# A hybrid decoder layer on one core: the local attention with heads paired over the key groups, the values as the stationary operand, and another order of VectorE's work

## The chip, the cores and the metric

The kernel runs on 1 core of one Trainium2 chip. The metric is the device time of one execution in microseconds (us), the median of three runs.

## The reference

One decoder layer on 256 tokens of width 1024. A gated linear attention (GLA) and a local attention (called SWA below) read the same normalised input; their outputs are gated, added and projected, and a mixture of 32 experts, 4 of them for each token, follows. The change is in the local attention:

```python
# q: 16 heads of 64, k and v: 2 key heads of 64, each shared by 8 query heads; window w = 128
scores = jnp.einsum('bnqhgd,bnkhd->bnhgqk', qb, kband) * (d ** -0.5)
scores = jnp.where(valid, scores, -jnp.inf)
m = jnp.maximum(jnp.max(scores, axis=-1, keepdims=True), sink)
p = jnp.exp(scores - m)
denom = jnp.sum(p, axis=-1, keepdims=True) + jnp.exp(sink - m)
out = jnp.einsum('bnhgqk,bnkhd->bnqhgd', p / denom, vband)
...
y_b = swa_with_sinks(q, k, v, sinks) @ w_swa_out
mixed = jax.nn.sigmoid(gate_a) * y_a + jax.nn.sigmoid(gate_b) * y_b
```

All numbers are float32. The dense products take each operand in two rounded parts (`_R` tiles) and make three products of them.

## The kernel before, in words

**Order of the program.** Each engine has its own queue, written out by hand, and the engines meet at semaphores. TensorE (PE) works through 19 blocks of dense products (`BLOCKS`), each in two units of weights (`kh` 0 and 1), each unit in two halves. SP loads a unit (`wblk`, 1 MB) once the unit five before it has been multiplied; ScalarE makes its high part (`split`), VectorE or GpSimd its low part (`rest`, or line 495 on GpSimd). From `gla_o` and `sw_out` on, SP also loads chunks of expert weights (`wexp`, 2 MB each, 192 in all) into the ring's tail. Then the experts run, 6 chunks for each; a chunk's place is filled again when TensorE has used it (`chunk_used`).

**The local attention** is cut in 8 groups (`NGRP`): for each of two blocks of 128 tokens (`i`), four groups of four heads (`g4`). Groups 0 to 3 have one tile of 128 keys, groups 4 to 7 two. Its steps are hooks inside the dense blocks 5 to 9. The hook of slot `n` runs `values(n - 2)`, `probs_t(n - 1)`, `scores(n)`, and after it TensorE goes on with dense products:

- `scores`: four products of 64 rows (the head width), two heads side by side on the upper and lower rows of the array, into PSUM banks 4 and 5.
- VectorE's `swa_mask` scales, masks, takes the maximum; ScalarE's `swa_exp` takes exponentials and their sums.
- `probs_t`: the probabilities are transposed, 4 or 8 transposes, and copied from PSUM to `PTS` by ScalarE and VectorE (`swa_pt`).
- `values`: for each head and key tile one product with the probabilities as the stationary operand (128x128) and the values as the moving one (64 columns), line 697, into bank 3.
- VectorE's `swa_out` adds up the denominator (line 1400), takes the reciprocal (1401) and multiplies (1404) into the token-major tile `SQR`.

After the last group `attention_t` transposes `SQR` with 16 transposes (`transpose16`, line 609) in block 10, and ScalarE and VectorE take high and low parts (`OB2`) for block `swao0`. VectorE's iteration `n` runs `swa_out(n - 2)`, `swa_pt(n - 1)`, `swa_mask(n)`, then evacuations of dense banks (line 1258), `rest` and GLA steps.

## Time and profile before

| | |
|---|---|
| median of 3 runs | 1206.51 us (1206.43 to 1206.67) |
| the profiled execution | 1206.25 us, its span 1204.4 us |
| granted TensorE clock | 0.999 |
| busy: PE, DVE, ACT, POOL | 1126.6, 378.2, 269.0, 148.8 us |
| memory read | 446.58 MB, 372 GB/s over the span |

How to read it: PE is TensorE, DVE is VectorE, ACT is ScalarE, POOL is GpSimd, SP the engine that issues most transfers. Busy time of PE is modelled (matmuls overlap), so the starts in the chain tell more than busy shares. The chain of waits is the one that ended last, followed back from the end: where two rows of it follow each other without a gap, the engine was never waiting. A float32 product is two instructions in the trace, a float32 transpose one.

### The profile page before, as it was taken

What the parts mean: (1) busy time and instruction counts of PE and PEld (TensorE: products, weight loads), DVE (VectorE), ACT (ScalarE), POOL (GpSimd) and SP (SyncE); (2) the same over time, 40 slices, a digit from 0 to 9 for tenths busy, and PEclk for the clock granted to TensorE, in tenths of its full rate; (3) what the DMA queues carried; (4) which work ended last, traced back from release to release, by engine and by line L of the source; (5) the groups of instructions that cost most, each with busy time, mean ns of one, the idle gap of its engine ahead of it and who ended that gap; (6) DMA issues with size and microseconds to landing.
All of it is one profiled execution on the core that took longest, in us unless ns stands there. A gap on an engine that the chain in (4) does not pass through costs nothing.

```text
span 1204.4 us, 17839 instructions
## 1 busy us (share of the span) xinstructions
PE 1126.6 (94%) x7411; PEld 558.7 (46%) x7411; DVE 378.2 (31%) x654; ACT 269.0 (22%) x410; POOL 148.8 (12%) x108
## 2 busy tenths in 40 slices
PE   7999999999999999999999999999999999998896
PEld 5988999984333333333333333333333333333332
DVE  6878744855211212211111111111111221111112
ACT  5465746332111111111111111111111111111112
POOL 6645543561000000000000000000000000000000
PEclk9999999999999999999999999999999999999999
DMA  7644336789999999999999999999999999999994
GB/s 295 215 172 158 106 141 243 295 309 375 414 393 426 429 429 426 428 429 429 428 428 428 429 429 429 428 428 429 428 429 428 428 429 429 428 428 429 428 429 204
DMA packets 35827, 448.14 MB, mean 372 GB/s; under 512 B 4160, under 2 KB 4288, under 8 KB 6576
## 3 DMA queue, kind: packets, MB, share of 16 engines
q1 hardware_dynamic: 34992, 445.99, 88.9%
q0 software_dynamic: 368, 1.24, 0.3%
q8 instruction: 26, 0.43, 0.1%
q10 hardware_dynamic: 432, 0.42, 0.1%
q14 instruction: 9, 0.07, 0.0%
HBM read 446.58 MB, written 1.05 MB: 372 GB/s over the span
## 4 chain that ended last, share of the span: by engine, by line
PE 51%; DMA 41%; DVE 4%; POOL 1%; ACT 1%; issue 1%; SPq 0%; DVEq 0%; ACTq 0%
DMA ring<-wexp 40%; PE PS L843 28%; PE PS L574 12%; PE PS L836 3%; PE PS L828 2%; POOL slot_R L495 1%; PE PS L904 1%; PE PS L697 1%; DVE slot_R L1203 1%; DMA ring<-wblk 1%; PE PS L671 1%; PE PS L820 0%; PE PS L684 0%; PE PS L609 0%; PE PS L899 0%
## 5 line engine op out<-in xcount | busy, mean ns | idle before, releaser
L843 PE MATMUL PS<-ring,SQ 128*64 128x512 f32 x2016 | 454.8, 596 | 58.0 <-DMA ring<-wexp 56.7
L843 PEld LDWEIGHTS PS<-ring,SQ 128*64 128x64 f32 x2016 | 138.3, 136 | 348.9 <-issue 227.8
L843 PE MATMUL PS<-ring,PTG 128*64 128x512 f32 x1024 | 226.8, 595 | 0.0
L843 PEld LDWEIGHTS PS<-ring,PTG 128*64 128x64 f32 x1024 | 70.7, 137 | 152.2 <-issue 133.2
L495 POOL TENSOR_TENSOR slot_R<-ring,slot_R 128x512 fp32r<-128x512 f32 (+1 forms) x80 | 124.2, 1584 | 96.2 <-ACT slot_R L948 96.2
L1641 DVE TENSOR_SCALAR SQ<-PS 128x512 f32<-128x512 f32 x32 | 22.1, 692 | 360.8 <-PE PS L843 360.8
L1149 ACT ACTIVATE SQ<-SQ 128x512 f32<-128x512 f32 x32 | 20.2, 630 | 494.0 <-DVE SQ L1641 494.0
L1632 DVE TENSOR_TENSOR PTG<-TAB,GRX 128x128 bf16<-128x128 f32 x32 | 9.3, 292 | 332.8 <-PE PS L891 332.8
L574 PE MATMUL PS<-slot_R 128*128 128x256 f32 (+1 forms) x296 | 92.3, 312 | 0.0
L948 ACT ACTIVATE slot_R<-ring 128x2048 fp32r<-128x2048 f32 (+1 forms) x38 | 71.6, 1888 | 41.5 <-DMA ring<-wblk 24.5
L836 PE MATMUL PS<-PTG,BRW 64*128 64x512 f32 x264 | 74.2, 640 | 0.7 <-ACT PTG L1157 0.7
L574 PE MATMUL PS<-HT_R,slot_R 128*128 128x256 f32 x400 | 73.3, 285 | 0.3 <-DVE GRX L1258 0.3
L1157 ACT ACTIVATE PTG<-PS 128x512 f32<-128x512 f32 x32 | 19.1, 597 | 208.2 <-PE PS L843 208.2
L574 PEld LDWEIGHTS PS<-HT_R,slot_R 128*128 128x128 f32 x400 | 62.3, 192 | 1.2 <-issue 0.7
L574 PE MATMUL PS<-slot_R,HT_R 128*128 128x512 f32 (+1 forms) x192 | 58.1, 378 | 0.7 <-POOL slot_R L495 0.7
L828 PEld LDWEIGHTS PS<-PTG,SQR 128*128 128x128 bf16 x1056 | 46.1, 98 | 26.0 <-issue 26.0
L574 PEld LDWEIGHTS PS<-slot_R 128*128 128x128 f32 x296 | 56.4, 191 | 2.9
L828 PE MATMUL PS<-PTG,SQR 128*128 128x64 bf16 x1056 | 50.0, 193 | 0.0
L828 PE MATMUL PS<-PTG,SIG 128*128 128x64 bf16 x528 | 47.8, 193 | 0.0
L1203 DVE TENSOR_TENSOR slot_R<-ring,slot_R 128x2048 fp32r<-128x2048 f32 (+1 forms) x17 | 43.5, 2560 | 8.3 <-ACT slot_R L948 8.1
L1149 ACT ACT_TABLE_LOAD x32 | 41.1, 1283 | 5.6 <-issue 5.1
L574 PEld LDWEIGHTS PS<-slot_R,HT_R 128*128 128x128 f32 x192 | 35.2, 188 | 9.2 <-POOL slot_R L495 1.1
(278 smaller groups left out, 991.3 us busy)
## 6 DMA issues: line engine op xcount, KB each, us to landing
ring<-wexp SPq DMA_DIRECT2D x190, 2048.0 KB, 33.3
ring<-wblk SPq DMA_DIRECT2D x36, 1024.0 KB, 4.8
EXT<-wexp SPq DMA_DIRECT2D x1, 2048.0 KB, 9.4
GRX<-wexp SPq DMA_DIRECT2D x1, 2048.0 KB, 12.2
BRW<-brow SPq DMA_DIRECT2D x7, 256.0 KB, 5.0
ring<-wskv SPq DMA_DIRECT2D x2, 768.0 KB, 10.3
GRX<-x SPq DMA_DIRECT2D x2, 512.0 KB, 4.3
out<-EXT SPq DMA_DIRECT2D x3, 256.0 KB, 2.0
```

The source lines that it names most:

```text
L495: last = nc.gpsimd.tensor_tensor(w_unit(u, True)[:, part], w_unit(u)[:, part], h_unit(u, True)[:, part].bitcast(F32), ALU.subtract)
L574: last = mm(dst, left(k, a), right(k, b), start=(kh == 0 and k == 0 and a + b == 0 and first), stop=(kh == 1 and k == KH - 1 and b == 1), ...
L671: last = mm(PS[:, 4 + hh % 2, (hh // 2) * SEQ:(hh // 2) * SEQ + ns], qT[p0:p0 + HD, h // 2, i * P:(i + 1) * P], KTT[p0:p0 + HD, h // (QH / ...
L697: last = mm(PS[:, 3, hh * HD:(hh + 1) * HD], PTS[:, n % 2, hh, st * P:(st + 1) * P], KVRAW[:, st, P + kv * HD:P + (kv + 1) * HD], start=(s ...
L828: last = mm(PS[:, 7, k * SLOTS:(k + 1) * SLOTS], XP[n // TT][:, n % TT, k * P:(k + 1) * P], SEL[:, n % TT, :], start=(n == 0), stop=(n == ...
L836: last = mm(bk(2 * i + n), SELT[rows, i * P:(i + 1) * P], Y[rows, :], start=False, stop=True, skip_group_check=True)
L843: last = mm(PS[g * SLOTS:(g + 1) * SLOTS, b, :], lhsT, rhs[:, g * 512:(g + 1) * 512], start=start, stop=stop)
L948: fn(h_unit(u, True), w_unit(u), ACT.Copy).then_inc(hi_ready, 1)
L1149: fn(SGM, GLU, ACT.Sigmoid, scale=ALPHA).then_inc(sgm_ready, 1)
L1157: fn(Y, bk(6), ACT.Copy).then_inc(y_ready, 1)
L1203: v.tensor_tensor(w_unit(u, True), w_unit(u), h_unit(u, True).bitcast(F32), ALU.subtract).then_inc(lo_v, 1)
L1641: v.tensor_scalar(GLU, bk(4), LIMIT, None, ALU.min).then_inc(glu_ready, 1)
```

## The change

Heads are paired over the two key heads: group `g4` now holds heads 2·g4 and 2·g4+1 of each key head, by a permutation of weight columns on the host. The score products are the same in number and size. The values become the stationary operand (128x64), and the transposed probabilities of two heads move (256 columns), the two key heads on the left and right halves of the array's columns. The output is then feature-major and needs no transposes at the end; but its division by the denominator needs the reciprocals spread over 64 features and transposed as well: VectorE writes them into `KD`, TensorE transposes them (two for each group), ScalarE copies the result to `KTT` (`swa_rb`), and VectorE multiplies. The keys no longer need a second copy, which takes away two transposes and four small writes.

```diff
-                kv = g4 // 2
-                for hh in range(HG):
-                    for st in range(i + 1):
-                        last = mm(PS[:, 3, hh * HD:(hh + 1) * HD], PTS[:, n % 2, hh, st * P:(st + 1) * P],
-                                  KVRAW[:, st, P + kv * HD:P + (kv + 1) * HD], start=(st == 0), stop=(st == i))
+                for st in range(i + 1):
+                    for kv in range(2):
+                        mm(PS[kv * HD:(kv + 1) * HD, 3, 0:2 * P], KVRAW[:, st, P + kv * HD:P + (kv + 1) * HD],
+                           PTS[:, n % 2, kv, 2 * st * P:2 * (st + 1) * P], start=(st == 0), stop=(st == i))
+                pe.wait_ge(sw_rd, n + 1)
+                for j in range(2):
+                    last = nc.tensor.transpose(PS[:, 3, (2 + j) * P:(3 + j) * P], KD[:, j, P:2 * P], ident)
                 last.then_inc(sw_o, 1)
...
-            def attention_t():
-
-                pe.wait_ge(sw_out, NGRP)
-                transpose16(lambda i, k: SQR[:, i, k * P:(k + 1) * P], obt_full)
-
             def gla_scores():
 
-                pe.wait_ge(obt_hi, 4)
-                pe.wait_ge(obt_lo, 4)
...
+            def swa_rb(n):
+                act.wait_ge(sw_o, n + 1)
+                if n:
+                    act.wait_ge(sw_out, n)
+                fn(KTT[:, 1, :], PS[:, 3, 2 * P:4 * P], ACT.Copy).then_inc(sw_rb, 1)
...
             for n in range(NGRP + 1):
+                if n >= 2:
+                    swa_rb(n - 2)
                 if 0 <= n - 1:
                     swa_pt(n - 1)
...
+            def swa_denominator(n):
+                q = n % 2
+                dve.wait_ge(sw_exp, n + 1)
+                link(v.tensor_tensor(S_DEN[q], S_SUM[q], S_ES[q], ALU.add))
+                link(v.reciprocal(S_RD[q], S_DEN[q]))
+                v.tensor_copy(KD[:, :, P:2 * P].rearrange("p j (v d) -> p j v d", v=2),
+                              S_RD[q].rearrange("p (v j) -> p j v", v=2).unsqueeze(3).broadcast_to([P, 2, 2, HD])).then_inc(sw_rd, 1)
+
             def swa_out(n):
                 i, g4 = n // (NGRP // TT), n % (NGRP // TT)
-                q = n % 2
-                dve.wait_ge(sw_exp, n + 1)
-                if n >= 2:
-                    dve.wait_ge(sw_out, n - 1)
-                link(v.tensor_tensor(S_DEN[q], S_SUM[q], S_ES[q], ALU.add))
-                link(v.reciprocal(S_RD[q], S_DEN[q]))
-                dve.wait_ge(sw_o, n + 1)
...
+                dve.wait_ge(sw_rb, n + 1)
+                v.tensor_tensor(OB_RAW[:, 2 * g4:2 * g4 + 2, i * P:(i + 1) * P],
+                                PS[:, 3, 0:2 * P].rearrange("p (j t) -> p j t", j=2),
+                                KTT[:, 1, :].rearrange("p (j t) -> p j t", j=2), ALU.mult).then_inc(sw_out, 1)
...
-                if n - 2 >= 0:
-                    swa_out(n - 2)
-                if 0 <= n - 1 < NGRP - 1:
+                if 0 <= n - 1 < NGRP:
                     swa_pt(n - 1)
                 if n < NGRP:
                     swa_mask(n)
+                if 0 <= n - 1 < NGRP:
+                    swa_denominator(n - 1)
+                if n - 2 >= 0:
+                    swa_out(n - 2)
...
-            dense(10, {(0, 1): [attention_t]})
+            dense(10)
```

The high and low parts of the attention's output are now each one instruction of 2048 columns from SBUF to SBUF (four of 512 from PSUM before), and block `swao0` waits for them.

On TensorE, slot 7 (in block 8) before. L574 are dense products, L697 the values, L684 the transposes of probabilities, L671 the scores; the numbers are output rows by columns.

```order
L574 MATMUL PS<-slot_R 128x512
L574 MATMUL PS<-slot_R,HT_R 128x512
L697 MATMUL PS<-GRX,ring 128x64 x8
L684 MATMUL PS<-TAB,ring 128x128 x8
L671 MATMUL PS<-KTT,SQ 128x256 x4
L574 MATMUL PS<-HT_R,slot_R 128x256 x2
```

The same place in the changed kernel (L575 dense, L694 values, L698 transposes of the reciprocals, L683 and L670 as L684 and L671).

```order
L575 MATMUL PS<-slot_R 128x512
L575 MATMUL PS<-slot_R,HT_R 128x512
L694 MATMUL PS<-ring,GRX 64x256 x4
L698 MATMUL PS<-TAB,GRX 128x128 x2
L683 MATMUL PS<-TAB,ring 128x128 x8
L670 MATMUL PS<-KTT,SQ 128x256 x4
L575 MATMUL PS<-HT_R,slot_R 128x256 x2
```

Eight products of 64 columns became four of 256, and two transposes came in behind them.

On VectorE, iteration 6 before: L1400, L1401 and L1404 are `swa_out(4)`, L1391 is `swa_pt(5)`, L1377 to L1386 are `swa_mask(6)`, L1258 the evacuation of a dense bank.

```order
L1400 TENSOR_TENSOR SM<-SM 128x4
L1401 RECIPROCAL SM<-SM 128x4
L1404 TENSOR_TENSOR SQR<-PS,SM 128x2x2x64
L1391 COPY ring<-PS 128x512
L1377 SCALAR_TENSOR_TENSOR ring<-PS,TAB 128x512 x2
L1382 TENSOR_REDUCE SM<-ring 128x4
L1384 TENSOR_TENSOR SM<-SM,ROW 128x4
L1385 TENSOR_SCALAR SM<-SM 128x4
L1386 TENSOR_TENSOR SM<-ROW,SM 128x4
L1258 TENSOR_TENSOR GRX<-PS,BRW 128x512
```

The same iteration in the changed kernel: L1396, L1397 and L1398 are `swa_denominator(5)`, L1404 is `swa_out(4)`, L1263 the evacuation.

```order
L1391 COPY ring<-PS 128x512
L1377 SCALAR_TENSOR_TENSOR ring<-PS,TAB 128x512 x2
L1382 TENSOR_REDUCE SM<-ring 128x4
L1384 TENSOR_TENSOR SM<-SM,ROW 128x4
L1385 TENSOR_SCALAR SM<-SM 128x4
L1386 TENSOR_TENSOR SM<-ROW,SM 128x4
L1396 TENSOR_TENSOR SM<-SM 128x4
L1397 RECIPROCAL SM<-SM 128x4
L1398 COPY GRX<-SM 128x2x128
L1404 TENSOR_TENSOR SQR<-PS,KTT 128x2x128
L1263 TENSOR_TENSOR GRX<-PS,BRW 128x512
```

The multiplication of group 4 moved from ahead of the mask to behind it, and a denominator (of the group after it) stands between the two.

## Rows read from the trace of the kernel before

**Rows 1.** Windows: busy us (instructions) of each engine, clock, DMA share, GB/s.

```profile
core 0: us, PE busy (x) PEld busy (x) DVE busy (x) ACT busy (x) POOL busy (x), PEclk, DMA share, GB/s
...
120.00:150.00 30.00, 30.00 (x224) 27.52 (x222) 22.36 (x37) 24.02 (x43) 15.55 (x13) 1.00 0.32 106
...
270.00:300.00 30.00, 28.33 (x231) 14.64 (x231) 14.26 (x52) 7.75 (x15) 4.64 (x4) 1.00 0.93 375
800.00:1100.00 300.00, 274.76 (x1778) 100.83 (x1778) 59.86 (x117) 36.44 (x53) 0.00 (x0) 1.00 1.01 428
```

**Rows 2.** Chain that ended last, attention stage: start us, us, what.

```profile
72.21 5.47 PE PS L574 x24
77.67 0.65 PE PS L671 x8
78.32 5.67 PE PS L574 x24
83.99 0.44 PE PS L684 x4
...
90.76 0.84 PE PS L697 x8
...
107.31 1.06 PE PS L671 x8
...
126.19 5.66 PE PS L574 x24
131.85 1.73 PE PS L697 x16
133.58 0.88 PE PS L684 x8
...
157.38 1.75 PE PS L609 x16
```

**Rows 3.** The same chain, 197 to 220 us.

```profile
197.68 14.41 PE PS L574 x120
...
212.11 6.90 DMA ring<-wblk
```

**Rows 4.** The same chain, expert stage.

```profile
287.31 10.30 PE PS L843 x48
...
302.38 10.88 PE PS L843 x52
...
500.40 31.69 DMA ring<-wexp
```

**Rows 5.** The same chain, 297 to 304 us.

```profile
299.68 1.06 PE PS L836 x4
300.74 0.59 PE PS L904 x4
```

**Rows 6.** The same chain: a step of one pass at 287.09 us.

```profile
287.09 0.22 PE PS L891 x2
```

**Rows 7.** Timeline of VectorE, 129 to 135 us: start, us, instruction [idle before].

```profile
129.01 1.15 DVE L1385 TENSOR_SCALAR SM<-SM 128x4 f32<-128x4 f32 x1
130.07 0.15 DVE L1386 TENSOR_TENSOR SM<-ROW,SM 128x4 f32<-128x4 f32 x1
...
130.74 0.67 DVE L1400 TENSOR_TENSOR SM<-SM 128x4 f32<-128x4 f32 x1
131.44 0.18 DVE L1401 RECIPROCAL SM<-SM 128x4 f32<-128x4 f32 x1
134.05 0.42 DVE L1404 TENSOR_TENSOR SQR<-PS,SM 128x256 f32<-128x256 f32 x1 [2.43 <-PE PS L697]
```

**Rows 8.** Timeline of GpSimd, 125 to 135 us.

```profile
125.10 5.02 POOL L495 TENSOR_TENSOR slot_R<-ring,slot_R 128x512 fp32r<-128x512 f32 x4 [4.38 <-ACT slot_R L948]
130.09 1.29 POOL L481 TENSOR_TENSOR GRX<-GRX,SIG 128x512 f32<-128x512 f32 x1
```

**Rows 9.** Groups of ScalarE instructions by form, 77 to 165 us: busy us, mean ns.

```profile
L1022 ACT ACTIVATE ring<-PS 128x256 f32<-128x256 f32 x4 | 1.5, 376 | 1.8 <-PE PS L684 1.8
```

More of the change, by code:

```diff
@@ L228, in program @@
         OB2 = (feature(SQ_R), feature(SQR_R))
+        OB_RAW = feature(SQR)
         OA2 = (feature(GV_R), feature(GR_R))
@@ L649, in _ @@
             pe.wait_ge(krot_ready, TT)
-            for g in range(2):
-                for i in range(TT):
-                    last = nc.tensor.transpose(PS[:, 3, (2 * g + i) * P:(2 * g + i + 1) * P],
-                                               KD[:, i, g * P:(g + 1) * P], ident)
+            for i in range(TT):
+                last = nc.tensor.transpose(PS[:, 3, i * P:(i + 1) * P], KD[:, i, 0:P], ident)
             last.then_inc(kt_full, 1)
@@ L668, in scores @@
                 for hh in range(HG):
-                    h = HG * g4 + hh
-                    p0 = (h % 2) * HD
-                    last = mm(PS[:, 4 + hh % 2, (hh // 2) * SEQ:(hh // 2) * SEQ + ns],
-                              qT[p0:p0 + HD, h // 2, i * P:(i + 1) * P],
-                              KTT[p0:p0 + HD, h // (QH // 2), 0:ns], start=True, stop=True)
+                    kv, j = hh % 2, hh // 2
+                    rows = slice(kv * HD, (kv + 1) * HD)
+                    last = mm(PS[:, 4 + kv, j * SEQ:j * SEQ + ns], qT[rows, 2 * g4 + j, i * P:(i + 1) * P],
+                              KTT[rows, 0, 0:ns], start=True, stop=True)
                 last.then_inc(sw_s, 1)
@@ L683, in probs_t @@
                     for st in range(i + 1):
-                        last = nc.tensor.transpose(PS[:, 6 + hh // 2, (2 * (hh % 2) + st) * P:(2 * (hh % 2) + st + 1) * P],
-                                                   SS[:, n % 2, hh, st * P:(st + 1) * P], ident)
+                        c = (2 * st + hh % 2) * P
+                        last = nc.tensor.transpose(PS[:, 6 + hh // 2, c:c + P], SS[:, n % 2, hh, st * P:(st + 1) * P], ident)
                 last.then_inc(sw_t, 1)
@@ L769, in _ @@
             for i in range(13, NB - 1):
+                if BLOCKS[i] == "swao0":
+                    pe.wait_ge(obt_hi, 1)
+                    pe.wait_ge(obt_lo, 1)
                 dense(i)
@@ L1069, in high_t @@
                     fn(dst[:, 2 * a:2 * a + 2, :], PS[:, 4 + a, :].rearrange("p (k t) -> p k t", k=2), ACT.Copy).then_inc(done, 1)
+            swa_rb(NGRP - 1)
             act.wait_ge(gr_ready, 3)
@@ L1074, in _ @@
             split(23)
-            high_t(OB2[0], obt_full, obt_hi)
+            act.wait_ge(sw_out, NGRP)
+            fn(OB2[0], OB_RAW, ACT.Copy).then_inc(obt_hi, 1)
             split(24)
@@ L1270, in rotate @@
                 link(v.tensor_tensor(t2, src[:, :, 1, :], s, ALU.mult))
-                for d in dst:
-                    last = v.tensor_tensor(d[:, :, 0, :], t1, t2, ALU.subtract)
-                link(last)
+                link(v.tensor_tensor(dst[:, :, 0, :], t1, t2, ALU.subtract))
                 v.tensor_tensor(t1, src[:, :, 1, :], c, ALU.mult)
                 link(v.tensor_tensor(t2, src[:, :, 0, :], s, ALU.mult))
-                for d in dst:
-                    last = v.tensor_tensor(d[:, :, 1, :], t1, t2, ALU.add)
-                last.then_inc(done, 1)
+                v.tensor_tensor(dst[:, :, 1, :], t1, t2, ALU.add).then_inc(done, 1)
                 dve.wait_ge(done, i + 1)
@@ L1352, in _ @@
                 evacuated(dve, 4 + i)
-                kd = KD[:, i, :].rearrange("p (h c x d) -> p h c x d", h=2, c=2, x=2)
                 rotate(KVRAW[:, i, 0:P].rearrange("p (h x d) -> p h x d", h=2, x=2),
-                       [kd[:, :, c] for c in range(2)], 2, i, krot_ready)
+                       KD[:, i, 0:P].rearrange("p (h x d) -> p h x d", h=2, x=2), 2, i, krot_ready)
             dve.wait_ge(z_ready, GH)
@@ L1692, in units, with head_pairs @@
         return w.reshape(2, KH, P, -1).transpose(0, 2, 1, 3).reshape(2, P, -1)
+    def head_pairs(a):
+        return a.reshape(2, QH // 2, HD, -1).transpose(1, 0, 2, 3).reshape(QH * HD, -1)
+    sq = slice(at["sq"], at["sq"] + QH * HD)
+    w_in, b_in = w_in.copy(), b_in.copy()
+    w_in[:, sq] = head_pairs(w_in[:, sq].T).T
+    b_in[sq] = head_pairs(b_in[sq])[:, 0]
     def columns(name):
@@ L1696, in columns @@
             w = f[{"gl": "w_gla_out", "sw": "w_swa_out", "wo": "w_out"}[name[:2]]][0]
+            if name[:2] == "sw":
+                w = head_pairs(w)
             n = int(name[-1]) * BW
```

34 lines of the change are left out of this document (12 added, 22 removed).

## The prediction

> **What bounds the kernel now.** I read the windows first, then the chain of waits from end to end, then the timelines of the engines in the attention stage. In the expert stage the transfers fill the DMA engines: share 1.01 at 428 GB/s, while PE is busy 275 of 300 us [rows 1], and the chain there is a product, then a transfer of over 30 us that it waited for, again and again [rows 4]. Ahead of the experts, from 270 to 300 us, the DMA share is 0.93 already. The chunks are issued as TensorE frees their places, so that stage is a block of fixed length whose start hangs on TensorE's arrival. The attention stage is another matter. The chain stays on PE there and its rows touch: the scores begin at 77.67 and last 0.65, the next dense row begins at 78.32 and lasts 5.67, the transposes begin at 83.99 [rows 2]. TensorE does not wait once from 70 to 212 us; then a transfer of weights, which was itself issued when TensorE had freed a unit at 212.1, takes 6.90 us [rows 3]. VectorE (22.36 of 30 us) and ScalarE (24.02) are well used beside it but end no wait [rows 1]. So a microsecond that TensorE saves before 160 us moves every later release with it, transfers of weights and chunks included, and the end too; what it must wait for is added in full.
>
> **The values, from the nearest rows.** A float32 product of 512 columns on half of the array's columns costs 10.30 / 24 = 0.429 us when two halves run at the same time: the row has 48 instructions, two for each product [rows 4]. The new products have 256 columns, so a pair (both key heads) takes 0.429 us. That is the stream alone. The rows also show a price for entering and leaving a split array. The scores (four products, 64 rows each) cost 0.65 us with 128 columns and 1.06 with 256: the stream is 0.41 for 128 columns and 0.24 is left over on entry [rows 2]. The dense row behind them takes 5.67 where the one behind plain transposes takes 5.47: 0.20 on leaving [rows 2]. Four transposes cost 0.59 behind a split product [rows 5] and 0.44 otherwise [rows 2]: 0.15. For entering the shape used here, the expert row of 52 instructions takes 10.88; 48 of them are worth 10.30, and four one-pass products 0.44 (0.22 for two [rows 6]), which leaves 0.14. I take 0.14 + 0.15 = 0.29 us for each group, since these two rows have the very shapes (columns halved; transposes behind it), with 0 and 0.44 as the ends.
>
> The Trainium skill, TensorEngine Tiling (Array Packing), Key Properties, says that a change of tiling mode drains the engine; the 0.14 to 0.24 us above agree. The same page, When to Use Tiling, advises exactly this swap for a moving side of 64 columns, at up to twice the speed; halving the old values and charging no drain gives 5.1 us there, where the rows give far less.
>
> Two transposes of the reciprocals are 0.22 us for each group (0.44 for four [rows 2]). Groups 0 to 3: 0.43 + 0.29 + 0.22 = 0.94 us in place of 0.84 [rows 2], 0.10 more each. Groups 4 to 7: 0.86 + 0.29 + 0.22 = 1.37 in place of 1.73 [rows 2], 0.36 less each. Sum over the eight: 0.4 - 1.44 = **-1.0 us**. The final 16 transposes go: **-1.75** [rows 2]. Two key transposes go: **-0.22**. TensorE's own work is 3.0 us less. With drains at 0.44 it is 1.8 less, with none 5.3 less.
>
> **The other engines.** ScalarE gets eight copies of 256 elements (0.38 us each [rows 9]) ahead of a copy that waits for later transposes anyway, hidden in its waits for VectorE. Scores, exponentials and probability copies keep their sizes. The high and low parts of the output wait for `sw_out` now, with blocks 10 to 14 ahead of their use: hidden. Fewer writes of rotated keys and a half-size key copy are off the path. No transfer is added.
>
> **The new wait.** `values(n)` cannot begin until `swa_out(n - 1)` has emptied bank 3. That was the first thing in VectorE's iteration; now it stands behind the mask and the denominator. Take TensorE's slot 7, which begins with `values(5)` at 131.85 [rows 2], 0.18 us earlier in the changed kernel by the terms above (0.22, less 4 x 0.10, plus 0.36): 131.67. VectorE ends the mask of group 6 at 130.22 [rows 7], and this end is tied to the scores. Then come the sum, the reciprocal (0.18), the spread copy (new; at most the 0.42 of a multiplication of 256 elements, at least a fraction of it) and the multiplication, 0.42 [rows 7]. Undisturbed, with 0.15 for the sum, as for its like at 130.07 [rows 7], and 0.1 between them, that is 131.5: 0.2 us to spare. But GpSimd works from 125.10 to 131.38 [rows 8], and VectorE's small instructions stretch at its borders: 1.15 us for one at 129.01, and the sum at 130.74 takes 0.67 and ends at 131.41, just behind GpSimd's instruction [rows 7, 8]. The Trainium skill, SBUF — State Buffer, SBUF: two separate sides, calls that an exclusive lock held for a whole instruction; the trace agrees with its 0.67 against 0.15. Put the new sum there and it too ends at 131.41. With 0.18, 0.42, 0.42 and 0.1 the bank is free at 132.5: TensorE waits **0.85 us**, and everything behind it, GpSimd's and ScalarE's next steps too, is that much later. In slots 1 to 5 GpSimd works less and the mask of one key tile is shorter; in slots 8 and 9 VectorE has no later mask or GpSimd is idle again, so I count one such wait. Its ends are 0 (no lock met) and 2.1 (the spread copy meets the next GpSimd instruction of 1.29 as well).
>
> **Sum.** -3.0 + 0.85 = -2.2 us. The profiled execution would go from span 1204.4 to 1202.2 (1206.25 to 1204.1 in all); its time is 0.26 under the median, so the median goes from 1206.51 to **1204.4 us**. A measurement of this kernel tells 0.2%, 2.4 us, from no change, so this is just within it.
>
> **The rivals.**
> - VectorE is in time: no wait of more than some tenths. For it: only the phase of GpSimd's instructions decides, and it shifts with ScalarE's splits. Against it: the stretched rows stand exactly there. -3.0 gives 1203.5 us, faster. Chance 0.32.
> - The drains cost nothing here, because the wait for the reciprocals or the loads cover them: -5.3, 1201.2 us, faster. Against it: each of four kinds of rows shows a drain. Chance 0.06. The advice in the Trainium skill, TensorEngine Tiling (Array Packing), When to Use Tiling, comes to the same time: 10.28 us of values halved is 5.1, less 1.76 of new transposes, plus 1.97 removed.
> - The late wait is larger (two locks, or drains at the upper end): -1.8 + 2.1 at worst, 1204.8 to 1206.8 us, no difference. Chance 0.09.
> - The halves do not run together: a pair costs 0.86. Groups 0 to 3 cost 0.53 more, 4 to 7 0.50 more, in all +4.1 - 2.0 + 0.85 = +3.0, 1209.5 us, slower. Against it: the expert rows run at 0.429. Chance 0.03.
> - The other side: VectorE's longer way back (mask, denominator, multiplication) is late in every slot of two key tiles, and TensorE waits at each `values`. It turns slower once these waits add up to 5.4 us (2.4 + 3.0), 1.1 in each of the five slots 5 to 9, for instance 1209.5 us at 6. It would need both locks in most slots, and GpSimd is busy only half of the time (15.55 of 30 [rows 1]). Chance 0.05.
>
> **How the numbers follow.** The forecast (a wait of 0.6 to 1.3 us, all within 0.2%) has 0.45. Faster by over 0.2%: 0.32 + 0.06 = 0.38. Slower: 0.03 + 0.05 = 0.08. Within: 0.45 + 0.09 = 0.54. The range takes in the forecast, the case without a wait (down to 1203.2) and most of the larger waits (up to 1206.2), about 0.84 together; the forecast's own range is 1203.9 to 1204.8.
>
> **What would show it.** In the chain after: the values with the two transposes 0.94 and 1.37 us in place of 0.84 and 1.73; no row of 16 transposes between 150 and 165 us; blocks 11 on some 2 to 3 us earlier than before, and the expert products with the same offset. In VectorE's timeline: the sum behind the mask stretched to over 0.5 us near 130 us and a gap on PE of just under 1 us ahead of the values of slot 7. The prediction is wrong if PE shows no such gap, or several, or if the pair of products takes 0.86 us, or if the expert stage does not start earlier by what the attention stage saved.

## The result, and the profile after

| | before | after |
|---|---|---|
| median | 1206.74 us (1206.15 to 1210.23, 20 runs) | 1209.14 us (1207.24 to 1211.60, 20 runs) |
| profiled execution, span | 1206.25, 1204.4 us | 1207.56, 1205.7 us |
| busy: PE, DVE, ACT, POOL | 1126.6, 378.2, 269.0, 148.8 us | 1123.7, 386.0, 271.0, 153.5 us |

The ratio is 1.0018, with a 95% interval of 1.0012 to 1.0024. The forecast was 1204.4 us, range 1203.2 to 1206.2: the time moved the other way, and out of the range.

TensorE's busy time fell by 2.9 us, as the sum had it. The chain of waits of after in the attention stage (start us, us, what) shows where the gain went first:

```profile
90.56 0.58 PE PS L694 x4
91.15 0.37 PE PS L698 x2
...
126.15 1.30 DVE ring L1377 x2
...
127.47 1.23 DVE SM L1382
...
129.54 1.22 DVE SM L1385
130.76 0.07 DVE SM L1386
130.83 1.19 DVE SM L1396
...
132.04 0.19 DVE SM L1397
...
132.29 1.12 issue
133.40 0.42 DVE SQR L1404
...
133.96 1.08 PE PS L694 x8
...
143.29 1.01 PE PS L694 x8
144.30 0.37 PE PS L698 x2
...
152.68 11.52 PE PS L575 x96
```

Values and transposed reciprocals take 0.58 + 0.37 = 0.95 us for one key tile (0.84 before) and 1.01 + 0.37 = 1.38 for two (1.73 before) [rows 2]. The last row, 96 dense instructions in one piece, has no transposes in its middle any more. But ahead of slot 7 the chain leaves TensorE and goes through VectorE from 126.15 to 133.82. VectorE's timeline there (start, us, instruction) shows which instructions are long:

```profile
128.73 0.78 DVE L1384 TENSOR_TENSOR SM<-SM,ROW 128x4 f32<-128x4 f32 x1
129.54 1.22 DVE L1385 TENSOR_SCALAR SM<-SM 128x4 f32<-128x4 f32 x1
130.68 0.15 DVE L1386 TENSOR_TENSOR SM<-ROW,SM 128x4 f32<-128x4 f32 x1
130.75 1.25 DVE L1396 TENSOR_TENSOR SM<-SM 128x4 f32<-128x4 f32 x1
132.04 0.18 DVE L1397 RECIPROCAL SM<-SM 128x4 f32<-128x4 f32 x1
132.25 1.23 DVE L1398 COPY GRX<-SM 128x256 f32<-128x256 f32 x1
133.40 0.41 DVE L1404 TENSOR_TENSOR SQR<-PS,KTT 128x256 f32<-128x256 f32 x1
```

GpSimd's timeline of the same stretch:

```profile
125.70 5.04 POOL L496 TENSOR_TENSOR slot_R<-ring,slot_R 128x512 fp32r<-128x512 f32 x4 [4.17 <-ACT slot_R L944]
130.69 1.29 POOL L482 TENSOR_TENSOR GRX<-GRX,SIG 128x512 f32<-128x512 f32 x1
132.06 1.27 POOL L485 TENSOR_TENSOR GRX<-GRX,ROW 128x512 f32<-128x512 f32 x1
```

The sum (L1396) begins at 130.75 and lasts until 131.98, where GpSimd's instruction of 130.69 ends; the spread copy (L1398) begins at 132.25 and lasts until GpSimd's of 132.06 has ended. Instructions of 128x4 take 0.15 to 0.2 us elsewhere in this list, and the spread copy takes 0.29 where nothing holds it (at 112.67 us in this trace). TensorE waits 2.2 us.

With that, the attention stage should still end 0.8 us earlier, and it ends 0.7 earlier: the 16 transposes of the linear attention's output begin at 195.25, before at 195.93. Yet the experts begin at 284.71 where they began at 283.44. The chain of after goes here through a transfer that did not stand in the chain of before [rows 3]:

```profile
195.25 1.75 PE PS L610 x16
197.00 2.89 PE PS L575 x24
199.89 0.28 issue
200.17 8.92 DMA EXT<-be
...
209.11 1.23 DVE BE L1243
```

It is the transfer of the experts' biases (`be`), which GpSimd issues when the gates are done and whose cast stands in VectorE's queue ahead of the low part of unit 30 and of an evacuation that TensorE waits for. The DMA view of this stretch (queue, kind: packets, MB, share of 16 engines; then issues with KB and us from issue to landing), first of the kernel before, 200.8 to 208.1:

```profile
q1 hardware_dynamic: 192, 1.84, 76.9%
...
EXT<-be POOLq DMA_DIRECT2D x1, 256.0 KB, 7.3
```

and of after, 200.1 to 209.1:

```profile
q1 hardware_dynamic: 223, 2.34, 81.9%
...
q8 instruction: 1, 0.02, 0.7%
...
EXT<-be POOLq DMA_DIRECT2D x1, 256.0 KB, 8.9
```

One packet of 16 KB on the queue named "instruction" is new in it, and the transfer takes 1.6 us longer. Before, a packet of this queue started at 198.7 us, ahead of the biases, and the next at 214.5, behind them; after, one starts at 187.2 and the next at 206.8.

What it does to TensorE shows in its waits from 200 to 230 us (engine, line, waited for: us, times, longest), before and after:

```profile
PE PS L574 <- DVE SIG L1500: 0.5, 1, 0.5
PE PS L575 <- DVE SIG L1497: 2.1, 1, 2.1
```

The cast of the biases begins at 209.11 in place of 208.15, and TensorE is 0.7 us ahead of before when it gets there, so it waits 1.6 us longer. One more wait for VectorE, near 254 us (line 1510 before, 1507 after), grew from 0.5 to 0.9. Together that is 2.0 us, which is what the stretch from the transposes to the experts lost (1.95).

### The profile page after: what moved, and what is told of

Same layout as the page of the kernel before. It is cut to its first block, busy times and chain, and to the rows that moved or that the text cites. A ratio compares the mean times of both kernels' runs of the same rounds, so it can differ in the third digit from the quotient of the medians.

```text
span 1205.7 us, 17737 instructions
## 1 busy us (share of the span) xinstructions
PE 1123.7 (93%) x7361; PEld 550.1 (46%) x7361; DVE 386.0 (32%) x655; ACT 271.0 (22%) x415; POOL 153.5 (13%) x108
## 4 chain that ended last, share of the span: by engine, by line
PE 50%; DMA 41%; DVE 5%; issue 1%; POOL 1%; ACT 1%; SPq 0%; DVEq 0%; ACTq 0%
DMA ring<-wexp 40%; PE PS L839 28%; PE PS L575 11%; PE PS L832 3%; PE PS L824 2%; POOL slot_R L496 1%; PE PS L900 1%; DMA EXT<-be 1%; DVE EXT L1245 1%; DVE slot_R L1208 1%; PE PS L670 1%; PE PS L694 1%; PE PS L816 0%; PE PS L683 0%; PE PS L895 0%
## 5 line engine op out<-in xcount | busy, mean ns | idle before, releaser
L496 POOL TENSOR_TENSOR slot_R<-ring,slot_R 128x512 fp32r<-128x512 f32 (+1 forms) x80 | 128.9, 1644 | 92.1 <-ACT slot_R L944 92.1
L575 PE MATMUL PS<-slot_R 128*128 128x256 f32 (+1 forms) x296 | 92.2, 312 | 0.0
L575 PE MATMUL PS<-HT_R,slot_R 128*128 128x256 f32 x400 | 73.2, 285 | 0.3 <-DVE GRX L1263 0.3
L575 PEld LDWEIGHTS PS<-HT_R,slot_R 128*128 128x128 f32 x400 | 62.3, 192 | 1.2 <-issue 0.7
L575 PE MATMUL PS<-slot_R,HT_R 128*128 128x512 f32 (+1 forms) x192 | 58.1, 378 | 0.7 <-POOL slot_R L496 0.7
L575 PEld LDWEIGHTS PS<-slot_R 128*128 128x128 f32 x296 | 56.4, 191 | 2.9
L575 PEld LDWEIGHTS PS<-slot_R,HT_R 128*128 128x128 f32 x192 | 35.1, 188 | 9.1 <-POOL slot_R L496 1.1
```

The costliest lines, as they stand in the source:

```text
L496: last = nc.gpsimd.tensor_tensor(w_unit(u, True)[:, part], w_unit(u)[:, part], h_unit(u, True)[:, part].bitcast(F32), ALU.subtract)
L575: last = mm(dst, left(k, a), right(k, b), start=(kh == 0 and k == 0 and a + b == 0 and first), stop=(kh == 1 and k == KH - 1 and b == 1), ...
```

## The experiments

Each kernel was timed beside the kernel before, and the ratio is to those executions of before, whose medians lie between 1206.6 and 1207.3 us; so kernels are better compared by their ratios than by their medians. The rows whose names begin with p, and x1p to x6p, have the padding that is explained below. Each line gives three stretches of the profiled execution besides the times, since they separate what the median mixes: S to T, from the dense row at 72 us (72.21 before [rows 2]) to the 16 transposes near 195 us, which is the attention stage; the landing time of the biases; and T to E, from those transposes to the experts' first products (283.44 before).

| kernel | median us (runs) | ratio, 95% interval | S to T | biases | T to E |
|---|---|---|---|---|---|
| before | 1206.74 (20) | | 123.72 | 7.30 | 87.51 |
| after | 1209.14 (20) | 1.0018, 1.0012 to 1.0024 | 123.23 | 8.92 | 89.46 |
| again | 1209.73 (11) | 1.0023, 1.0014 to 1.0032 | 124.97 | 9.26 | 89.83 |
| x1_no_lock | 1205.70 (11) | 0.9998, 0.9989 to 1.0007 | 120.86 | 8.89 | 89.48 |
| x2_out_first | 1214.52 (5) | 1.0059, 1.0045 to 1.0073 | 128.35 | 9.16 | 91.22 |
| d1_late_biases | 1208.28 (11) | 1.0010, 1.0001 to 1.0019 | 125.03 | | 88.35 |
| x3_den_first | 1208.02 (11) | 1.0010, 1.0001 to 1.0019 | 122.34 | 8.84 | 89.43 |
| r1_order_alone | 1207.30 (11) | 1.0005, 0.9995 to 1.0014 | 124.72 | 7.55 | 87.98 |
| p1_changed_padded | 1207.99 (11) | 1.0005, 0.9996 to 1.0014 | 124.91 | 7.47 | 87.83 |
| p0_before_padded | 1207.25 (11) | 1.0003, 0.9994 to 1.0012 | 123.72 | 7.43 | 87.50 |
| x1p_no_lock_padded | 1203.85 (11) | 0.9979, 0.9970 to 0.9988 | 120.90 | 6.79 | 87.19 |
| x3p_den_first_padded | 1206.23 (11) | 0.9998, 0.9989 to 1.0007 | 123.47 | 7.25 | 87.67 |
| x3pd_late_biases | 1207.44 (11) | 1.0008, 0.9999 to 1.0017 | 123.52 | | 89.76 |
| p0b_before_36 | 1209.91 (7) | 1.0027, 1.0016 to 1.0039 | 124.04 | 8.43 | 89.00 |
| p0c_before_28_8 | 1208.72 (11) | 1.0018, 1.0009 to 1.0027 | 124.07 | 8.98 | 89.55 |
| x4_short_pool | 1207.30 (11) | 0.9997, 0.9988 to 1.0006 | 122.42 | 9.02 | 89.84 |
| x4p_short_pool_padded | 1205.40 (11) | 0.9987, 0.9978 to 0.9996 | 122.42 | 7.12 | 87.40 |
| x5p_shorter_pool | 1216.57 (5) | 1.0072, 1.0058 to 1.0085 | 130.59 | 7.7 | 90.58 |
| x6p_short_where_needed | 1205.61 (11) | 0.9987, 0.9978 to 0.9996 | 122.07 | 7.5 | 87.87 |

**The changed kernel once more, and why its times scatter.**

> The changed kernel once more, unchanged. Theory A (VectorE's lateness in slot 7, plus the late landing of the expert biases): slot 7 again shows a gap of about 2 us on PE ahead of the values, the GLA transposes (16 in one row, near 195 us) begin about 0.7 us earlier than before, and what is lost behind them depends on how long the bias transfer takes: 1207.2 us when it lands by 208, 1209 to 1211 when it lands later. Rival B (nothing to do with the program, the chip's transfers alone): the gap in slot 7 is not there again, or the ratio to the kernel before is 1.000.

Its profile has the same gap, and behind it something that after's profile had not. Its windows (us, busy us of PE, PEld, DVE, ACT, POOL, granted clock, DMA share, GB/s):

```profile
134.00:136.00 2.00, 1.73 (x11) 1.10 (x12) 0.72 (x2) 1.98 (x2) 0.00 (x0) 0.76 1.00 422
136.00:138.00 2.00, 2.00 (x11) 1.67 (x11) 0.09 (x1) 1.43 (x4) 0.84 (x1) 0.50 0.10 37
```

and its chain behind the gap:

```profile
134.27 1.27 PE PS L694 x8
135.54 0.62 PE PS L698 x2
136.16 1.71 PE PS L683 x8
137.87 1.37 PE PS L670 x8
```

The granted clock falls from 1.00 to 0.50, that is from 2.4 to 1.2 GHz, after TensorE has stood still for 2.2 us, and the four steps take 4.97 us where after took 1.08 + 0.37 + 0.87 + 1.06 = 3.38. The profiles with a gap of 2.2 us in slot 7 show the fall in three cases of four (again, d1, p1; not in after), and so does that of x5p_shorter_pool behind a wait of 7.4 us. The mean granted clock of every execution is on record too, and it splits the changed kernel's 20 times in two: the 6 between 1207.2 and 1208.0 us have 0.998, the 14 from 1208.99 us on have 0.996 or 0.997. In those of before that were timed beside the experiments it is 0.997 once in 131 and 0.998 or 0.999 in all others. Every profile with a fall has a mean of 0.997 or less and every one without has 0.998 or more, so the clock falls in most executions of the changed kernel. Where it falls only the profiled ones show, and slot 7 is not the only place (see the end of this section).

**Is it GpSimd that holds VectorE?** Its work beside slots 6 and 7 is left out:

```diff
+                w = 8 if u == 14 else BW
+                part = GR[:, m, n * BW:n * BW + w]
...
+                        if u in (17, 18, 19):
+                            last = nc.gpsimd.memset(w_unit(u, True)[:, part].bitcast(F32), 0.0)
+                            continue
                         last = nc.gpsimd.tensor_tensor(w_unit(u, True)[:, part], w_unit(u)[:, part],
```

> The changed kernel with GpSimd nearly idle while slots 4 to 7 run: it leaves out the low parts of the weights of units 17, 18 and 19 (a memset in their place) and all but 8 columns of the gating of unit 14. VectorE's order is the changed one. Theory A, in its part on GpSimd: the two stretched instructions of swa_denominator near 131 us fall back to 0.15 and 0.29 us, the gap in slot 7 is gone or under 0.3 us, GLA transposes near 193.1 us. Rival D (the length of VectorE's chain of instructions alone decides, GpSimd does not matter): the gap stays at 1 us or more.

VectorE's timeline of this kernel at the same place:

```profile
128.87 0.17 DVE L1389 TENSOR_SCALAR SM<-SM 128x4 f32<-128x4 f32 x1
...
129.03 0.16 DVE L1400 TENSOR_TENSOR SM<-SM 128x4 f32<-128x4 f32 x1
...
129.43 0.29 DVE L1402 COPY GRX<-SM 128x256 f32<-128x256 f32 x1
```

Every instruction that was held here is short again, TensorE waits for nothing in the attention stage, and the attention stage is 2.86 us shorter than before: the sum's 3.0 less the 0.2 that lies ahead of S. So TensorE's terms were right, and the gap is GpSimd's doing. But the profiled execution gained 0.8 us only (1205.44 against 1206.25): T to E is 89.48, as in the changed kernel. The second loss has nothing to do with the gap.

**VectorE's order.** Two attempts to let VectorE be in time by order alone, first the output ahead of everything:

```diff
+                if n - 2 >= 0:
+                    swa_out(n - 2)
                 if 0 <= n - 1 < NGRP:
                     swa_pt(n - 1)
...
-                if n - 2 >= 0:
-                    swa_out(n - 2)
```

> The changed kernel with one move: VectorE runs swa_out(n - 2) first in its iteration again, as in the kernel before, then the copy, the mask and the denominator. Theory A: the gap in slot 7 is gone, since bank 3 is emptied before the mask begins; the GLA transposes begin at 193.0 us, 2.2 earlier than in the changed kernel and 2.9 earlier than before (195.93). The end follows in full if the rest of the program hangs on TensorE alone: 1203.6 us, 0.9976 of the time before; it follows in part if the bias transfer decides (about 1205 to 1207). Rival C (the multiplication only moves its wait: VectorE now stands at swa_rb with the mask behind it): scores and exponentials come later, PE waits at the transposes of probabilities or the scores instead, and the GLA transposes stay at 195 us.

Waits of its VectorE (engine, line, waited for: us, times, longest):

```profile
DVE SQR L1404 <- ACT KTT L1024: 16.7, 6, 5.0
```

ScalarE's copy of the transposed reciprocals stands behind its exponentials, a split of 1.9 us and table loads of 1.28 us, and now the next group's mask, from which those exponentials come, stands behind that copy: a loop through both engines. The swap of the operands needs the mask ahead of `swa_out`. What that order costs without the swap:

> The kernel before with VectorE's new order alone (copy, mask, sum and reciprocal, multiplication), the heads, the values and the final transposes as before. Theory A: the old denominator is two small instructions with no spread copy, and no ScalarE copy stands ahead of the multiplication, so the bank is late by at most one hold of GpSimd: a gap of 0 to 1 us in slot 7, 1206.5 to 1207.7 us. Rival G (the order by itself costs what the change lost): 1209 us.

A wait of 0.7 us for `swa_out` in slot 7; the median rose by 0.6 us, within the interval of no change. The denominator ahead of `swa_pt` and the mask, with `KD`'s two halves in turn:

```diff
                 if 0 <= n - 1 < NGRP:
+                    swa_denominator(n - 1)
                     swa_pt(n - 1)
```

> The changed kernel with swa_denominator(n - 1) at the head of VectorE's iteration, where VectorE waits for the transposed probabilities anyway (1.9 us ahead of the copy in slot 7), and with the spread reciprocals written to the two halves of KD in turn, so that it need not wait for TensorE; copy, mask and multiplication follow as in the changed kernel. All work is done. Theory A' (what makes TensorE wait is the denominator with its two instructions held up by GpSimd, which stands between the mask and the multiplication that frees bank 3): no gap of PE in slots 6 and 7 over 0.3 us, no drop of its clock, the GLA transposes begin at 192.9 us, as in the kernel with an idle GpSimd (192.95), and the time is 1205.0 to 1206.0 us. Rival F (GpSimd's holds move on to the mask's own small instructions, and the bank stays late): a gap of 1 us or more stays, 1207 us or more.

The gap at `values` is gone and the clock stays at 1.00, but the denominator's spread copy met GpSimd in other slots (1.14 us, at 94.0 and 109.1), the mask behind it was later, and TensorE waited 0.5 us for the exponentials ahead of the transposes of the probabilities. From S to T 0.9 us came back, and T to E stayed at 89.43.

**What happens behind the attention.** Two theories: VectorE's queue (the cast of the biases stands ahead of what TensorE needs), or the fetch of TensorE's program. For the first, the cast is moved behind the evacuation of block 13:

```diff
             rest_t(OA2, oat_full, oat_lo)
-            biases1(0)
             rest(30)
...
                 if i == 13:
+                    biases1(0)
                     biases2(0)
```

> The changed kernel with biases1(0) (VectorE's first piece of work on the expert biases, which waits for their transfer) moved behind the low part of unit 30 and the evacuation of block 13. The slot 7 gap of 2.2 us stays. Theory A, in its part on the biases: VectorE no longer holds up unit 30 and bank 2 behind the transfer, the wait of PE at 213.5 to 216.3 us goes, and 1 to 2 us come back: 1205.8 to 1206.8 us, and its times scatter less than those of the changed kernel. Rival E (VectorE has the same work until 254 us in either order, so that stage is as long): 1207.5 to 1209 us, scattered as before.

T to E shrank from 89.83 to 88.35: part of the loss came back. TensorE then waits for other work of VectorE (0.9 us for line 1516), which has the casts to do later on. For the second, TensorE's program is made 112 instructions longer ahead of the first block, by products of one element:

```diff
                 banks = [pj_bank(), pj_bank()]
+                for _ in range(28):
+                    mm(PS[0:1, 2, 0:1], TAB[:, T_ONE:T_ONE + 1], TAB[:, T_ONE:T_ONE + 1], start=True, stop=True)
```

> The changed kernel with 28 products of one element on TensorE (112 instructions) ahead of its first block, where it waits for weights. Each 16 KB of TensorE's program is fetched by one transfer; in the changed kernel, with 100 instructions fewer by then, one such fetch starts at 206.8 us, inside the transfer of the expert biases (200.2 to 209.1), in the kernel before it started at 198.7, ahead of it (200.9 to 208.2). Theory H (the fetch holds up one of the 16 engines and with it the biases): the fetch moves to about 198.5, the bias transfer takes 7.3 to 7.9 us from its issue in place of 8.9 to 9.3, and VectorE's first bias instruction comes 1.3 to 1.6 us earlier against TensorE's GLA transposes than in the changed kernel; about 1 us in the end, 1208.5 us. Rival I (the biases wait for the chunk issued 0.1 us behind them, and the fetch is chance): 8.9 us as before.

The fetch moved from 206.8 to 199.9 us, ahead of the biases. The DMA view of that transfer, 201.8 to 209.3, has no "instruction" line:

```profile
q1 hardware_dynamic: 198, 1.93, 78.5%
...
EXT<-be POOLq DMA_DIRECT2D x1, 256.0 KB, 7.4
```

T to E fell by 1.6 us to 87.83, and TensorE's wait behind the biases from 2.1 to 0.6. The gap in slot 7 stayed, with a fall of the clock behind it as in again.

> The kernel before with the same 28 products of one element. The fetch that started at 214.5 us now comes some 7 us earlier, inside the bias transfer. Theory H: the bias transfer takes 8.8 to 9.3 us in place of 7.3, and the kernel becomes 0.8 to 1.5 us slower, about 1207.9 us. Rival I: 7.3 us and 1206.8 us.

The forecast failed: the fetch came at 209.1 us, 0.6 behind the landing and not inside the transfer, so this run could not show a loss, and showed none. It does show that the 28 products by themselves cost nothing that can be told here (ratio 1.0003). With more products:

> The kernel before with 36 of the one-element products ahead of its first block (144 instructions; 28 of them put the fetch at 209.1 us, 0.6 us behind the end of the biases' transfer). Here the fetch should start near 207.5 us, inside that transfer. Theory: the transfer takes 8.5 to 8.9 us in place of 7.3, block swao0 begins about 1 to 1.3 us later than 253.4, and the median rises to near 1207.8 us, ratio 1.001, with no other change. Rival: the place of the fetch is of no account, the transfer takes 7.4 us as with 28 products, ratio 1.0003 or less.

The transfer took 8.43 us and T to E 89.00, but TensorE's start was late too (S at 74.63 us, 72.37 with 28 products): its first 16 instructions of 512 columns took 3.78 and 3.07 us for each eight, against 2.14 and 1.99 with 28. What differs is the clock, and not the 36 products. The trace's first record of the full clock stands at 19.2 us in this execution, at 10.5 in the one with 28, and nothing is on record ahead of it, where the windows print 1.00. The instructions behind that moment are at full speed. The profiled executions of r1_order_alone and d1_late_biases, which have no padding, and of x1p and x6p, which have 28 products, show the same up to 16 us (3.4 to 3.8 us for the first eight). So this lateness is in the profiled execution's time and says nothing on the fetch. The next one has eight of the products behind the first block instead:

> The kernel before with 28 one-element products ahead of the first block and 8 more behind it, ahead of block 1, where TensorE waits 0.7 us for GpSimd anyway. With 36 ahead of the first block TensorE's start was 2.2 us later as well, which hid what the place of the fetch costs; here the start should be at most 0.3 us later. Theory: the fetch falls near 207.6 us into the transfer of the biases, which takes 8.4 to 8.9 us (7.4 with 28 alone), block swao0 begins 1.0 to 1.5 us later than 253.4, median near 1208.0 us, ratio 1.001. Rival: the loss of the run with 36 was all its late start, and this one is at 1207.2 us as with 28.

S is at 72.20 as before. The DMA view, 201.1 to 210.2:

```profile
q8 instruction: 1, 0.02, 0.7%
...
EXT<-be POOLq DMA_DIRECT2D x1, 256.0 KB, 9.0
```

This is the kernel before, with nothing of the change in it, and 36 one-element products give it the whole loss behind the attention: 8.98 us for the biases, a wait of 2.1 us behind them, T to E 89.55, ratio 1.0018 (S to T is 0.35 us longer as well, without a wait of TensorE above 0.3 us). The rival (all was the late start) fell.

**Both causes taken away.**

> The changed kernel with GpSimd nearly idle in the middle of the attention stage (a memset in place of the low parts of units 17 to 19, gating of unit 14 in 8 columns: work left out), and 28 one-element products ahead of the first dense block, which cost TensorE nothing that it does not wait for anyway there but make its program 112 instructions longer. Theory: the full gain of the change, 3.0 us at the transposes of the linear attention, is seen at the end once the fetch of TensorE's program no longer falls into the transfer of the expert biases: that transfer takes 7.5 us (8.9 without the products), block swao0 begins near 250.5 us (252.4 without them, 253.4 in the kernel before), span near 1201.5, median near 1203.5 us, ratio to the kernel before 0.9975. Rival: the biases' transfer is not what is lost behind the attention stage, and the time stays at the 1205.7 us measured without the products.

1203.85 us: what the sum without a wait gave (1203.5), in a kernel that leaves work out.

> The changed kernel with the denominator of a group ahead of the probability copy and the mask, the shifted reciprocals in the two halves of the key copy in turn, and the 28 products of the padding. Complete computation. Without the products this one had no gap in slot 7 and measured 1208.0. Theory: the biases take 7.5 us in place of 8.8, block swao0 begins near 252.2 (253.8 without the products), span near 1203.3, median near 1206.3 us, ratio 0.9995. Rival: the products change nothing, 1208.0 us.

The median is as expected, the attention stage is not: S to T is 123.47 against 122.34 without the padding. The order on VectorE is the same, but with everything 0.1 us later a third small instruction of the mask met GpSimd (1.32 us at 131.85, where it took 0.15 before), and a gap of 0.8 us at `values` came back. So it was in part luck of a tenth of a microsecond that x3_den_first had no gap. Moving the biases as well lost 1.2 us of medians: T to E is 89.76 and TensorE waits up to 1.8 us for line 1517, the other work that now stands behind the casts. The two intervals overlap a little.

> The previous but one (denominator first, 28 products) with VectorE's cast of the expert biases of the first expert moved behind the evacuation of block 13 as well. Complete computation. Theory: VectorE then waits for no bias transfer at all, so block swao0 begins another 0.3 to 0.8 us earlier than without this move, near 251.7; median near 1205.8 us, ratio 0.9991. Rival: the cast is not on the path any more once the transfer is short, and this run is within 0.3 us of the one without the move.

**Short GpSimd instructions, all of the work done.**

```diff
+                w = BW // 4
+                for a in range(0, BW, w):
+                    last = nc.gpsimd.tensor_tensor(part[:, a:a + w], part[:, a:a + w],
+                                                   SIG[:, m * BW + a:m * BW + a + w], ALU.mult)
...
-                    quarter = unit_width(u) // 4
-                    for n in range(4):
+                    parts = 8 if u >= 14 else 4
+                    quarter = unit_width(u) // parts
+                    for n in range(parts):
```

> The changed kernel with GpSimd's work in the attention stage cut into shorter instructions: low parts of the units from 14 on in eighths in place of quarters, each gating step in four pieces of 128 columns. All is computed, and GpSimd does the same number of elements. Theory: what costs in slot 7 is that each of VectorE's small instructions is held for the rest of one GpSimd instruction of 1.25 us; with instructions of 0.65 and 0.35 us the gap of 2.2 us falls to under 1.2, so the transposes of the linear attention begin near 194.0 us (195.25 in the changed kernel, 192.95 with GpSimd idle). The fetch still falls into the transfer of the biases (8.9 us), so the median is near 1206.6 us, ratio 1.0000. Rival: the hold goes by how long GpSimd is at work in all, and the gap stays at 2 us or more, 1208 to 1209 us.

> The same with the 28 products of the padding, so that the fetch of TensorE's program leaves the transfer of the biases. All is computed. Theory: both losses are gone, and what is left of the gap is about 1 us: median near 1204.8 us, ratio 0.9984, faster than the kernel before and the changed one. Rival: gap as before, 1207 us.

VectorE's timeline of the padded one:

```profile
130.65 0.78 DVE L1404 TENSOR_TENSOR SM<-SM 128x4 f32<-128x4 f32 x1
...
131.68 0.30 DVE L1406 COPY GRX<-SM 128x256 f32<-128x256 f32 x1
131.90 0.41 DVE L1412 TENSOR_TENSOR SQR<-PS,KTT 128x256 f32<-128x256 f32 x1
```

and waits of its TensorE:

```profile
PE PS L702 <- DVE SQR L1412: 0.6, 1, 0.6
PE PS L581 <- POOL slot_R L502: 0.5, 1, 0.5
```

The hold follows the length of GpSimd's single instructions: the gap is 0.6 us, though GpSimd is busy longer in all (5.6 us in place of 5.04 for the low parts of 2048 columns). With the padding, 1205.40 us, ratio 0.9987 with an interval of 0.9978 to 0.9996, is a little faster than the kernel before, and by ratios 0.3% faster than the changed one (1.0018). Twice as short again was too much:

> The same again with sixteenths (256 columns) and gating in eight pieces of 64 columns. Theory: the hold is shorter still, 0.3 us or less for each small instruction, gap in slot 7 under 0.7 us, 1204.3 us, but GpSimd's own overhead for the many instructions may eat it up: not over 0.5 us on either side of the run with eighths. Rival: no difference from the quarters.

Its chain through GpSimd's many small instructions:

```profile
138.93 6.43 POOL GRX L490 x8
...
150.94 12.81 POOL slot_R L502 x16
```

TensorE waited 7.4 us for GpSimd. And the shorter instructions only where VectorE's attention work is beside them:

> The kernel with short GpSimd instructions and the padding, with the eighths only where VectorE works beside them on the attention (units 17 to 19) and quarters again for the units behind; gating in four pieces as before. All is computed. With eighths everywhere GpSimd's low parts of the units behind took 23.3 us for 24 instructions where quarters took 15.1 for 8 of twice the size and 3.7 for 3, and TensorE waited 0.5 us for them at 157.4. Theory: this wait goes and the rest stays: transposes of the linear attention near 194.0 us, median near 1204.9 us, ratio 0.9983. Rival: the wait at 157.4 is of no account for the end, because something later is waited for anyway: 1205.4 us as with eighths everywhere.

The wait for GpSimd is gone, S to T is 0.35 us shorter, the ratio the same: the rival came true.

**Where else the clock falls.** TensorE's wait behind the biases is a standstill of 2.0 to 2.4 us when the fetch falls into the transfer (1.6 in p0b; 2.2 also in x5p, whose transfer was short but whose first cast took 2.6 us). The profiles of x2_out_first and x4_short_pool show a fall of the clock behind that wait. Windows of x4_short_pool, in the standstill and behind it:

```profile
213.40:215.40 2.00, 0.07 (x1) 0.00 (x0) 2.00 (x2) 0.43 (x1) 0.00 (x0) 1.00 1.02 426
218.00:220.00 2.00, 2.00 (x11) 2.00 (x11) 1.02 (x1) 0.00 (x0) 2.00 (x2) 0.51 1.02 434
```

Behind the same wait the profiles of after, again, p0c, x1, x3 and x5p show none, so it does not come each time. Counted over all executions, by their mean granted clock:

| standstills of TensorE in the profile, behind 130 us | kernels | executions at 0.997 or less |
|---|---|---|
| 2.2 us in slot 7 and 2.1 to 2.4 behind the biases | after, again | 14 of 20, 9 of 11 |
| 2.2 us in slot 7 alone | d1, p1 | 8 of 11, 7 of 11 |
| 2.0 to 2.2 us behind the biases alone | x1, x3, x4, p0c | 5, 6, 6, 5 of 11 |
| none above 0.8 us | r1, p0, x1p, x3p, x4p, x6p | 0, 0, 0, 0, 1, 2 of 11 |

So both standstills bring such executions, and the kernel before gets them from 36 products alone (p0c). They are longer: 1209.6 against 1207.5 us by medians in the changed kernel.

## Why the prediction was wrong

1. **TensorE's terms.** Values -1.0, transposes -1.75 and -0.22: right. x1_no_lock measures -2.86 from S to T besides the key transposes. The drains taken from rows of before (0.29 for each group) hold: 0.95 and 1.38 us measured against 0.94 and 1.37.
2. **The place and kind of the new wait**: right, one gap ahead of `values` in slot 7, and by GpSimd's hold.
3. **"TensorE waits 0.85 us"**: the mechanism was right, the size was 2.2. The mask was to end at 130.22, since its end was taken as tied to the scores; it ended at 130.83, as its instruction of line 1384 was held as well (0.78 us, 0.16 before). The sum was to end at 131.41 and ended at 131.98, since it met the next GpSimd instruction from its start. The spread copy was priced at 0.42 and took 1.15 until the multiplication could begin, held by the GpSimd instruction behind. I had put this at the end of the bounds ("the spread copy meets the next GpSimd instruction as well"), and had given that case 0.09. A held instruction ends with GpSimd's, so the one behind it starts where the following GpSimd instruction has just started. Four instructions were held here in after (lines 1384, 1385, 1396 and 1398), three in r1_order_alone and x3p_den_first_padded at the same place, and two in x3_den_first: the case at the end of the bounds was a common one. The Trainium skill, SBUF — State Buffer, SBUF: two separate sides, has the lock go to whichever starts first and be kept for the whole instruction; for a VectorE instruction with two inputs from this memory it names only a GpSimd instruction that reads it. The runs agree: the two-input instruction on `ring` (line 1345) that took 1.78 us beside GpSimd's subtraction at 106.6 us of after took 0.69 beside a GpSimd memset in x1_no_lock.
4. **What a standstill does to the clock** was not in the sum at all. A fall in slot 7 adds 1.6 us to the four steps behind it. The changed kernel's 6 executions at a clock of 0.998 have a median of 1207.5 us, 0.8 above before; its 14 others pull the median to 1209.1. In which of the two places the clock fell in these is not known, but each place alone brings such executions.
5. **"A microsecond that TensorE saves before 160 us moves every later release with it"**: this is the step that failed. It held up to 197 us. It did not hold for the transfer of the biases, because fetches of TensorE's own program share the DMA engines with it and go by the count of instructions, not by the work. The changed kernel has 44 matmul instructions fewer in the windows up to 199 us (1313 against 1357), each with its weight load, which put a fetch into the transfer. That cost 1.95 us from T to E, more than the 0.7 us that TensorE had kept. Shown by four pairs with and without the padding (p1 against after: 1.6; x1p against x1: 2.3; x3p against x3: 1.8; x4p against x4: 2.4 us of T to E, the last with a fall of the clock in it; TensorE's wait behind the biases is 2.0 to 2.2 us in the four without and 0.5 to 0.8 in the four with the padding) and by p0c on the kernel before (2.0).

The books of the profiled execution, in which the clock did not fall: -3.0 + 2.2 + 1.95 = +1.15; measured +1.3 of span. The "other side" that I priced (VectorE late in every slot) did not come; the rise came from two causes, neither of which decides alone, and from the clock behind both. Of the one that I had not seen, the profile of before shows its part: packets of the queue named "instruction" stand in its DMA view, and the biases' cast waits 7.95 us for the transfer in VectorE's timeline.

Open: why the first products run at half speed until 16 to 19 us in some executions; why the clock falls behind some standstills of 2.0 to 2.4 us and not behind others; and by what path one 16 KB packet delays a transfer by 1.5 us. That it does is shown, the path is not.

## What to carry to other kernels

A change that takes away instructions also moves every fetch of that engine's program. Where a small transfer stands alone on the critical path, look in the DMA view for an "instruction" packet inside it, before and after; a few idle instructions at a place where the engine waits anyway may be worth more than the change. And when VectorE's small instructions stand beside a train of long GpSimd instructions, price every one of them at up to the length of a GpSimd instruction, not at its own. Shorter GpSimd instructions shorten the holds, but GpSimd's work grows with their number: halves helped here, quarters made TensorE wait for GpSimd.

## What the runs showed of the hardware

- **Instruction fetch is in the way of small transfers.** A 16 KB packet on the "instruction" queue inside a 256 KB transfer came with 8.4 to 9.3 us in place of 6.8 to 7.7, in every one of the 17 profiles in which both can be told. 36 products of one element moved it in (p0c). The Trainium skill, Runtime: NRT & Kernel Launch, Instruction fetch mechanics, describes such fetches in blocks of 256 instructions and calls their cost mostly hidden. The size of the packet, 16 KB, agrees; the distance does so roughly: TensorE has 265 instructions between the packets at 198.7 and 214.5 us of before, and 335 between those at 187.2 and 206.8 of after. The cost here was near 2 us, by way of another's transfer.
- **A held VectorE instruction ends with GpSimd's**: 128x4 instructions of 0.15 us took 1.22 and 1.25 in after beside GpSimd instructions of 1.26 to 1.29, and at most 0.78 in x4p_short_pool_padded beside ones of 0.70.
- **Short GpSimd instructions cost GpSimd**: four of 512 columns took 5.04 us, eight of 256 took 5.6, sixteen of 128 took 6.8 (after, x4_short_pool, x5p_shorter_pool).
- **A standstill of 2.2 us can halve TensorE's clock** behind it (granted clock 0.50 from 135 to 139 us in again, with 11 matmul instructions from 136 to 138 us where after has 17). It did so behind 5 of 12 standstills of 2.0 to 2.4 us ahead of the experts in the profiles, and never behind those of 1.8 us and less there. Executions at a lower mean clock are 3 of 66 in the kernels without a wait above 0.8 us, and 22 of 44 in those with one of 2.0 to 2.2 us behind the biases.
